# The two heads of a pair as one chain, with their matmuls side by side, in three attentions of 64-wide heads

## Time and profile before

| | us |
|---|---|
| three runs | 2573.09, 2574.38, 2575.44 |
| median | 2574.38 |
| the profiled execution | 2571.84 |
| its span | 2570.1 |
| PE busy | 2461.1 (96%) |
| DVE busy | 1205.6 (47%) |
| ACT busy | 898.8 (35%) |
| POOL busy | 479.7 (19%) |

### The profile page before, as it was taken

One profiled execution on the slowest core, in us unless ns is written; L12 is line 12 of the kernel. 1 busy time (PEld: TensorE's weight loads), 2 busy tenths in 40 slices (PEclk: granted clock), 3 DMA queues, 4 the chain that ended last, 5 costly groups with the idle time before them and its releaser, 6 DMA issues.

```text
span 2570.1 us, 29822 instructions
## 1 busy us (share of the span) xinstructions
PE 2461.1 (96%) x11676; PEld 1912.5 (74%) x11676; DVE 1205.6 (47%) x1922; ACT 898.8 (35%) x1412; POOL 479.7 (19%) x323
## 2 busy tenths in 40 slices
PE   6999999999999999899999999999999999999997
PEld 5666666888888888677777777766678887788886
DVE  4332444444544435665565641455544445444444
ACT  5323446322322223433333432344433444322222
POOL 3111211000201102434333434000001201100001
PEclk8889999999999999999999999999999999999999
DMA  4211211223223222211111112222122331223222
GB/s 166 74 41 51 65 50 50 91 90 95 94 97 99 92 93 96 83 50 42 42 42 50 34 42 74 98 66 66 50 79 93 126 113 58 90 99 97 94 96 75
DMA packets 56763, 199.21 MB, mean 78 GB/s; under 512 B 6304, under 2 KB 6432, under 8 KB 56240
## 3 DMA queue, kind: packets, MB, share of 16 engines
q1 hardware_dynamic: 56624, 197.30, 23.3%
HBM read 195.13 MB, written 2.15 MB: 77 GB/s over the span
## 4 chain that ended last, share of the span: by engine, by line
PE 51%; DVE 4%; ACT 2%; issue 1%; POOL 1%; DMA 0%; ACTq 0%; DVEq 0%; POOLq 0%; SPq 0%
PE bank L956 13%; PE bank L911 13%; PE bank L962 12%; PE bank L958 12%; DVE ya L1701 2%; PE bank L914 1%; DVE gv L1704 0%; ACT whi L1344 0%; ACT obh L1480 0%; DVE gk L1704 0%; ACT bdpt L1494 0%; POOL wlo L2141 0%; ACT sqb L1378 0%; ACT cwt L1378 0%; DMA memx<-in_mem2T 0%
## 5 line engine op out<-in xcount | busy, mean ns | idle before, releaser
L956 PE MATMUL bank<-hh,whi 128*128 128x512 f32 x1680 | 703.4, 419 | 25.9 <-ACT whi L1344 16.9
L962 PE MATMUL bank<-hh,wlo 128*128 128x512 f32 x1680 | 672.4, 400 | 2.7 <-DVE wlo L1701 2.4
L958 PE MATMUL bank<-hl,whi 128*128 128x512 f32 x1680 | 671.7, 400 | 0.7 <-DVE hl L1704 0.7
L1344 ACT ACTIVATE whi<-stage 128x1024 fp32r<-128x1024 f32 x340 | 357.2, 1051 | 401.1 <-PE bank L962 394.3
L1701 DVE TENSOR_TENSOR wlo<-stage,whi 128x1024 fp32r<-128x1024 f32 x260 | 343.9, 1323 | 302.6 <-ACT whi L1344 302.4
L956 PEld LDWEIGHTS bank<-hh,whi 128*128 128x128 f32 x1680 | 321.6, 191 | 107.5 <-ACT whi L1344 17.1
L962 PEld LDWEIGHTS bank<-hh,wlo 128*128 128x128 f32 x1680 | 320.2, 191 | 83.4 <-DVE wlo L1701 5.6
L958 PEld LDWEIGHTS bank<-hl,whi 128*128 128x128 f32 x1680 | 321.4, 191 | 70.8 <-issue 3.1
L2141 POOL TENSOR_TENSOR wlo<-stage,whi 128x1024 fp32r<-128x1024 f32 x80 | 193.5, 2419 | 523.1 <-ACT whi L1344 523.1
L911 PEld LDWEIGHTS bank<-ya 128*128 128x128 f32 x1024 | 129.6, 198 | 14.5 <-issue 6.2
L911 PE MATMUL bank<-ya 128*128 128x128 f32 x1024 | 137.7, 285 | 1.4 <-DVE ya L1701 1.4
(11 more groups left out here) (363 smaller groups left out, 3644.9 us busy)
## 6 DMA issues: line engine op xcount, KB each, us to landing
stage<-in_wall SPq DMA_DIRECT2D x340, 512.0 KB, 3.7
gbc<-rows SPq DMA_DIRECT2D x8, 512.0 KB, 4.3
band<-in_toep SPq DMA_DIRECT2D x16, 256.0 KB, 4.5
x<-in_xT SPq DMA_DIRECT2D x8, 256.0 KB, 5.7
fb<-rowsf SPq DMA_DIRECT2D x8, 256.0 KB, 3.6
out_y<-fout SPq DMA_DIRECT2D x8, 256.0 KB, 2.2
cft<-in_cf SPq DMA_DIRECT2D x1, 1344.0 KB, 10.1
memx<-in_memT SPq DMA_DIRECT2D x1, 1024.0 KB, 4.8
```

The lines of the kernel that those rows point to most:

```text
L956: pe.matmul(o, wh, hi, start=j == 0, stop=False)
L958: pe.matmul(o, wh, lo, start=False, stop=False)
L962: i = pe.matmul(o, wl, hi, start=False, stop=end)
L1344: act.activation(k.whi[u % NSPLIT][:], k.stage[u % NSTAGE][:], ACT.Copy).then_inc(*up("whi", u))
```

## The change

`sb_head` and `soft_head`, one generator for each head, become `sb_pair` and `soft_pair`, one for each pair. Their steps hold what the two heads' steps held, head 0 before head 1. Three steps of TensorE are written anew, and take both heads: the scores of either kind, and the value sums of either kind. They first wait for what both heads need, and then issue head 0 and head 1 alternately, block by block. In the stick-breaking and fox scores the mask matmuls of both heads come behind all score matmuls. The turns stay one for each head, and come behind the scores of both. No instruction of the other engines is changed, added or moved.

```diff
+    def sb_pair(self, p):
+        two = []
+        for hh in range(2):
...
+            two.append(Head(h, "sb", p, hh, u, "osb"))
+        yield [st("sb_z", two, *(o.uses[b] for o in two for b in range(3)))]
+        yield [st("sb_ln", o, o.uses["A"]) for o in two]
         yield []
         yield []
+        yield [st("sb_sp", o) for o in two]
         for s in (3, 2, 1, 0):
+            yield [st("sb_cum", (o, s)) for o in two]
+        yield [st("sb_w", o, o.uses["W"]) for o in two]
         yield []
+        yield [st("sb_o", two, *(o.uses["o"] for o in two))]
+        yield [st("out", o) for o in two]
...
+    def soft_pair(self, kind, p, place, src):
...
+        yield [st("sm_s", (two, 0), *(o.uses["z", 0] for o in two))]
         for b in range(4):
+            yield [st("sm_max", (o, b), o.uses["zb", b], o.uses["st", b]) for o in two]
+            yield [st("sm_exp", (o, b), o.uses["p", b]) for o in two]
+            nxt = [st("sm_s", (two, b + 1), *(o.uses["z", b + 1] for o in two))] if b < 3 else []
+            yield nxt + [st("sm_turn", (o, b), o.uses["tb", b], o.uses["pt", b]) for o in two]
+            yield [st("sm_pv", (two, b, use), *([use] if b == 0 else []))]
+        yield [st("out", o) for o in two]
...
-            yield from par(*(self.sb_head(p, hh) for hh in range(2)), nxt)
+            yield from par(self.sb_pair(p), nxt)
...
-            yield from par(*(self.soft_head("fox", p, hh, "fx", "ofx") for hh in range(2)), *back[p])
+            yield from par(self.soft_pair("fox", p, "fx", "ofx"), *back[p])
...
+    def sb_scores(two):
+        p = two[0].i
+        s2 = p % 2
         wait(("dve_ev", ("w_in", 128 * p, 0)), ("dve_ev", ("w_in", 512 + 128 * p, 0)), ("cb", 0))
+        for o in two:
+            for s in range(3):
+                free(o.uses[s])
         for s in (0, 1, 3, 2):
+            for o in two:
+                r = slice(64 * o.hh, 64 * o.hh + 64)
+                mm(sb_regions(o)[s], k.k[s2][r, blk[s]], k.q[s2][r, 128 * s:T], s != 3, False)
+        for o in two:
+            for s in (0, 1, 3, 2):
+                i = mm(sb_regions(o)[s][:, 0:128], k.cb("ident"), k.cb("strict"), False, False)
+            i.then_inc(*up("pe_z", o.no))
...
+    def sb_values(two):
+        v = k.v[two[0].i % 2]
+        wait(("act_turn", ("w_in", 1024 + 128 * two[0].i)))
+        for o in two:
+            free(o.uses["o"])
+            wait(("act_w", (o.no, 2)))
         for s in range(4):
+            n = T - 128 * s
+            for o in two:
+                r = slice(64 * o.hh, 64 * o.hh + 64)
+                i = mm(bank[2 + 3 * o.hh][r, 128 * s:], v[:, s, r], k.sbW[o.hh][:, woff[s]:woff[s] + n], s == 0, s == 3)
+                if s == 3:
+                    i.then_inc(*up("pe_o", o.no))
...
+    def soft_scores(two, b):
...
+        for o in two:
+            free(o.uses["z", b])
+        for o in two:
+            r = slice(64 * o.hh, 64 * o.hh + 64)
+            i = mm(bank[2 + o.hh][:, 0:n], q[r, blk[b]], kk[r, 0:n], True, not fox)
+            if not fox:
+                i.then_inc(*up("pe_s", (o.no, b)))
+        if fox:
+            for o in two:
+                i = mm(bank[2 + o.hh][:, 128 * b:n], k.cb("ident"), k.cb("causal"), False, True)
+                i.then_inc(*up("pe_s", (o.no, b)))
...
+    def soft_values(two, b, use):
...
+        for o in two:
+            pe.wait_ge(*at("sm_t", (o.no, b)))
         for s in range(b + 1):
+            for o in two:
+                r = slice(64 * o.hh, 64 * o.hh + 64)
+                i = mm(bank[6][r, blk[b]], v[:, s, r], soft_bufs(o)[4][:, blk[s]], s == 0, s == b)
+                if s == b:
+                    i.then_inc(*up("pe_pv", (o.no, b)))
```

More of the change, by code:

```diff
@@ L503, in fox_forget @@
         yield [st("ff_row", u, u)] + [st("fox_rows", (h, fb[h]), fb[h]) for h in range(4)]
-    def soft_head(self, kind, p, hh, place, src):
-        h = (kind, p, hh)
-        u = {"o": Use("b6", [(n, (src, p, x)) for n in ("o_hi", "o_lo") for x in range(2)])}
-        for b in range(4):
[L509 to L523, removed]
+    def soft_pair(self, kind, p, place, src):
+        two = []
+        for hh in range(2):
+            h, u = (kind, p, hh), {}
+            for b in range(4):
+                u["z", b] = Use(f"b{2 + hh}", [("sm_mx", (h, b))])
+                u["zb", b] = Use(f"{place}zb{hh}", [("sm_p", (h, b))])
+                u["st", b] = Use(f"{place}st{hh}", [("sm_n", (h, b))])
+                u["p", b] = Use(f"{place}p{hh}", [("pe_pt", (h, b))])
+                u["pt", b] = Use(f"{place}pt{hh}", [("pe_pv", (h, b))])
+                u["tb", b] = Use(f"b{4 + hh}", [("sm_t", (h, b))])
+            two.append(Head(h, kind, p, hh, u, src))
+        use = Use("b6", [(n, (src, p, x)) for n in ("o_hi", "o_lo") for x in range(2)])
+        yield [st("sm_s", (two, 0), *(o.uses["z", 0] for o in two))]
+        for b in range(4):
+            yield [st("sm_max", (o, b), o.uses["zb", b], o.uses["st", b]) for o in two]
[4 more added lines that the diff above has]
+        yield [st("out", o) for o in two]
@@ L781, in block2 @@
                 yield from band_loads(p + 1)
-            yield from par(*(self.soft_head("band", p, hh, "bd", "ob") for hh in range(2)),
-                           *([proj(p + 1)] if p < 7 else []))
+            yield from par(self.soft_pair("band", p, "bd", "ob"), *([proj(p + 1)] if p < 7 else []))
         yield [st("fence", "mg2")]
@@ L1038, in soft_bufs @@
         return q, kk, v, P, PT
[L1040 to L1044, removed]
-        else:
[L1046 to L1051, removed]
+    def soft_scores(two, b):
+        n, fox, p = 128 * b + 128, two[0].kind == "fox", two[0].i
+        q, kk, _, _, _ = soft_bufs(two[0])
+        if fox:
+            wait(("hn_out", ("fq", p)), ("hn_out", ("fk", p)))
+        else:
+            wait(("dve_ev", ("w_in_2", 4112 + 128 * p, 0)), ("dve_ev", ("w_in_2", 5136 + 128 * p, 0)))
+        for o in two:
[5 more added lines that the diff above has]
+                i.then_inc(*up("pe_s", (o.no, b)))
+        if fox:
+            for o in two:
+                i = mm(bank[2 + o.hh][:, 128 * b:n], k.cb("ident"), k.cb("causal"), False, True)
+                i.then_inc(*up("pe_s", (o.no, b)))
     def soft_turn(o, b):
@@ L1059, in soft_turn @@
         i.then_inc(*up("pe_pt", (o.no, b)))
[L1061 to L1064, removed]
+    def soft_values(two, b, use):
+        p, v = two[0].i, soft_bufs(two[0])[2]
         if b == 0:
[L1066 to L1069, removed]
+            wait(("act_turn", ("w_in", 2560 + 128 * p) if two[0].kind == "fox" else ("w_in_2", 6160 + 128 * p)))
+            free(use)
+        for o in two:
+            pe.wait_ge(*at("sm_t", (o.no, b)))
         for s in range(b + 1):
-            i = mm(out, v[:, s, pb:pb + 64], PT[:, blk[s]], s == 0, s == b)
-        i.then_inc(*up("pe_pv", (o.no, b)))
+            for o in two:
[3 more added lines that the diff above has]
+                    i.then_inc(*up("pe_pv", (o.no, b)))
     half = [bank[7][:, NM * j:NM * j + NM] for j in range(2)]
```

36 lines of the change are left out of this document (5 added, 31 removed).

## The result

The changed kernel takes 2501.06 us (median of four, 2500.41 to 2502.62), beside 2573.74 for the kernel before on the same chip (2571.31 to 2575.44): a ratio of 0.9725, 95% interval 0.971 to 0.9739. The forecast was 2506. The two profiled executions have spans of 2570.1 and 2500.8 us, so 69.3 us went.

| stage | before | after | difference | forecast |
|---|---|---|---|---|
| stick-breaking pair 0 | 41.85 | 32.17 | -9.68 | -9.65 |
| pair 1 | 41.86 | 32.16 | -9.70 | -9.65 |
| pair 2 | 40.37 | 32.17 | -8.20 | -8.25 |
| pair 3 | 50.38 | 43.65 | -6.73 | -6.75 |
| fox pairs 0 to 3 | 198.96 | 188.03 | -2.85, -2.67, -2.83, -2.58 | -3.0, -2.5, -2.3, -3.8 |

What follows compares the result with a forecast made beforehand. TensorE, busy for 96% of the span, was taken to bound the kernel. Banded 22.5, stick-breaking 34 and fox 11.5 sum to 68 us: 2571.84 profiled becomes 2504, with 2.5 for the median 2506; forecast band 2496 to 2512, range 2494 to 2523.

Steps and rivals of the forecast that it cites:

- Stick-breaking scores: First score to running sums: 7.3 us gained in pair 2, 8.7 in pairs 0 and 1, 5.8 in pair 3.
- Why the clock doesn't fall: Behind stick-breaking scores: over 5 us of half-array matmuls, one head at a time, becomes 2.3 us with both halves working.
- Rival (a): Clock still falls in the stick-breaking scores: about 30 us of dips cost 13 us, giving 2519; chance 0.14.
- Rule against the change: Matmuls start and end strictly first in, first out; four passes take three slots, not two; about 2518 us.
- Rival (b): Wide side-by-side score matmuls, 512 columns, don't keep pace: 2518 to 2526, at the far end 2545; chance 0.12.
- Value sums and outputs: Stick-breaking pairs gain 0.95 us each; banded pairs gain 0.26 in block 2, lose 0.49 by the joint wait.
- Banded pairs: Scores and sums side by side: 2.7 us in each of seven pairs, 3.5 in the last, 22.5 in all.
- Fox pairs: Scores and sums side by side: 3.0, 2.5, 2.3 and 3.8 us gained in the four pairs, together 11.5.
- Rival (c): Chains absorb the gain, joint waits striking where slack was seen: one microsecond in each of 16 pairs, 2522; chance 0.14.
- (d): Slower than before: the clock falls once in each fox and banded pair, 12 costing 82 us, 2600; chance 0.02.
- (e): Pairs don't run side by side at all, only joint waits of 8 x 0.5: about 2573; chance 0.01.
- the last sign: Sign against the prediction, in the changed kernel's profile: clock slices 2 to 4 still show 8.

Runs made afterwards that it cites:

- values_only: Changed kernel with scores back in the old order, head after head, a mask behind each block; value sums stay side by side: 2572.58 us, ratio 1.0008.
- scores_only: Changed kernel with value sums issued head after head, each head with its own waits; scores stay side by side: 2506.07 us, ratio 0.9748.
- apart_long: Changed kernel with stick-breaking scores head after head, masks behind each head's passes, and four more overwritten score blocks per head: 2533.18 us, ratio 0.9857.
- apart: Changed kernel with stick-breaking scores strictly head after head, each head's masks behind its own passes: 2511.09 us, ratio 0.9771.
- head_after_head: Changed kernel with all stick-breaking score passes of head 0 before those of head 1, masks behind both: 2509.7 us, ratio 0.9765.
- masks_inside: Changed kernel with the two stick-breaking masks behind each block's side-by-side passes instead of all masks behind all passes: 2504.55 us, ratio 0.9747.
- more_scores: Changed kernel with four more overwritten blocks of side-by-side passes ahead of the stick-breaking scores: 2512.66 us, ratio 0.9777.

## Why the prediction was right, and where its reason was not

**What bounds the kernel: right.** TensorE's saved time appears in full in every pair; VectorE and ScalarE took over nowhere for long.

**Stick-breaking scores: right in size.** Forecast 7.3 us in pair 2 and 8.7 in pairs 0 and 1. The old order costs 4.32 at full clock and the rest is the clock's. The forecast had 2.9 us from the first score to the projection (2.79 measured), of which 0.6 for the masks (0.43). Taking apart the 9.68 of pair 0: side by side against strictly apart 2.45 - 0.31 = 2.14; seven trips fewer at 0.31, 2.2; the value sums and outputs 0.93; and 10.2 us of half clock that are gone, 3 x 1.47 = 4.4. Sum 9.67. (The first two are the 4.32 parted by the price of a trip, so what the sum tests is 4.32 and 1.47 from values_only and 0.93 from scores_only, against the kernel before.) With 10.2, 6.8 and 3.4 us for pairs 1, 2 and 3, the differences of the table come out within 0.05. So of the 34.3 us of this attention 13.2 are the clock's.

**Why the clock doesn't fall: the outcome right, the reason wrong.** The step that failed is "what TensorE did before it fell was over 5 us of half-array matmuls, one head at a time". It was read in pair 2, where the clock fell 5.95 us behind the first score. In pairs 0 and 1 it fell after 4.33 and 3.44 us already:

```profile
121.08:124.52 3.44, 3.44 (x13) 1.49 (x12) 0.00 (x0) 0.00 (x0) 1.74 (x1) 1.00 0.17 38
124.52:134.76 10.24, 10.24 (x23) 5.55 (x23) 3.24 (x6) 4.39 (x4) 0.00 (x0) 0.50 0.11 40
```

And it was not the cause: the longer such stretch in apart_long left the clock up. That the clock stayed at full in the changed kernel was, as far as the stated reason goes, luck: the change also gathered the masks. The cause lies in the masks between the passes; values_only has them and its clock falls. Rival (a), built on the same reason, was priced well for a dip (1.4 us for 3.4; values_only shows 1.47) but made to depend on the wrong thing. TensorE shows as busy without a gap in both kinds of stretch (4.80 of 4.80 us before the fall, 10.95 of 10.95 with none), so the busy column alone doesn't tell them apart. The Trainium skill (TensorE: Matmul & The Clock Gate, Part 1: The HAM clock gate) ties the clock to how busy TensorE has been; the busy column here neither bears that out nor refutes it. What in the alternation lowers the clock stays open. Head 0's passes and masks take 3.58 us in the kernel before (162.94 to 166.52, by the single records) and 2.68 in apart (79.70 to 82.38): whether the 0.9 us lost on the trips is what counts, no run tells. The masks behind each block with both halves at work (four trips, 3.7 us) left it up; one half alone with as few trips, or both halves with eight, wasn't tried.

**Rule against the change: the runs decide.** Four wide passes of two heads take the time of two (1.06 us), not of three, and head 1's first pass starts 0.53 us ahead of head 0's second, which stands before it in the program. So the rule of strictly ordered starts and ends doesn't hold between row halves here, and the 2518 that followed from it didn't come. The run head_after_head bears out the reading of the value sums of block 2 too: passes of the other half do start over waiting ones, but in both cases only when three are left.

**Rival (b) is gone** with the same row: 512 columns keep pace as 128 do. The choice of the near end of the range (1.06) was right.

**Value sums and outputs: right.** 0.93 for 0.95 in a stick-breaking pair; the joint wait 0.56 for 0.49. With 0.26 of gain in block 2 these two make +0.30 a banded pair, and values_only has 31.38 against 31.11 before, +0.27.

**Banded pairs: right**, 2.67 for 2.7, with 1.69 for the forecast 1.7 in the step of block 3's scores. The last pair gave 3.03 for 3.5, but it can't be read so finely: at an identical program it took 24.27 us in one execution and 24.89 in the other, with 10.2 and 13.7 us of half clock.

**Fox pairs: the sum right (10.9 for 11.5), the parts not.** Pair 2 gave 2.83 for 2.3. Pair 3 gave 2.58 for 3.8. The seven executions with the same fox part (the changed kernel twice, masks_inside, head_after_head, more_scores, apart, apart_long) took 51.5 to 52.4 us there, and the table has the longest; by the shortest it is 3.5. So up to 0.9 of the 1.2 is scatter. What the rest is stays open. Head 1's turn in pairs 1 and 2 has the idle time foretold (1.35 and 1.36 us). Rival (c), a microsecond absorbed in each of 16 pairs, didn't come: only pair 3 is more than 0.5 us short of its forecast.

**Rivals (d) and (e): no.** The change made the clock fall in no fox or banded pair. But the prediction's reading that these run at 1.00 left out fox pair 3, which has 6.8 us of half clock in both kernels, around waits of TensorE of up to 2.47 us. Before, and after:

```profile
397.70:451.20 53.50, 48.19 (x238) 34.47 (x237) 20.25 (x62) 31.30 (x62) 10.35 (x5) 0.94 0.16 50
```

```profile
355.77:408.17 52.40, 46.32 (x243) 33.99 (x243) 21.37 (x64) 32.04 (x64) 10.40 (x5) 0.93 0.15 51
```

Two slips beside: four microseconds later than 2574 is 2578, and not the 2573 of rival (e); and the slices that showed 8 before are the first three, so of the slices 2 to 4 in the last sign only two could change.

**The median:** 5 us under the forecast. 1.3 are the sum's (69.3 for 68: the pairs gave 0.6 less than forecast, and 1.9 went outside them, where the two programs are alike and the forecast had nothing), and the profiled execution lay 1.6 above its median, where I had added 2.5 by the kernel before.

## What to carry to other kernels

Issue matmuls of the two row halves, or column halves, in turn, one of the one and one of the other: here passes of 512 columns then cost half, while the same passes one head after the other overlapped only at the seam. Gather the full-array matmuls between them into one group: each trip between half array and full array cost 0.3 us here, and a tight alternation of the two brought TensorE to 1.2 GHz for 3.4 to 10.2 us a pair. In the stick-breaking attention that was worth more (13.2 us) than the scores side by side (4 x 2.14 = 8.6). Where two chains are made one, look at what their joint wait delays behind them: one output instead of two, and the copy that TensorE waits for first, gave back another 0.28% together.

## What the runs showed of the hardware that I had not expected

- The half clock doesn't need a TensorE that looks idle, nor a long half-array stretch: 10.95 us of single halves, with masks twice, kept 2.4 GHz; single halves with a mask behind each block's passes lost it 3.4 to 6.5 us behind the first, in eight pairs of eight.
- A pass of the other row or column half started ahead of waiting ones when three of them were left, not earlier (head_after_head, and the value sums of the kernel before); interleaved, the passes of the two halves start 0.007 us apart.
- A trip from 64-row fp32 passes to a full-array mask and back costs 0.31 to 0.32 us by two differences: masks_inside, and values_only less apart (there once the half clock is taken out at 1.47 us for 3.4).
- How long the half clock lasts varies at one and the same program: 6.8, 3.4, 6.8 and 10.2 us in the four pairs of one execution of values_only. A difference of 1.5 or 3 us in a pair can be no more than that.
